# Routed expert outputs summed into one row per token by an accumulating indirect DMA

## The reference, cut to what matters

```
def hier_moe(h, ...):                 # h: 2048 x 1024
    grp    = argmax(h @ w_rg + b_rg)              # one of 4 groups
    gate_g = softmax(...)[grp]
    top_v, top_i = top_k(logits of the group's 8 experts, 2)
    w_top  = softmax(top_v) * gate_g[:, None]     # two weights per token
    expert = grp * 8 + top_i                      # 2 of 32 experts
    ...                                           # pairs sorted by expert, padded to blocks of 128
    def expert_block(tok, e):                     # 128 tokens of one expert
        xb  = h_pad[tok]
        hid = silu(xb @ w_gate[e]) * (xb @ w_up[e])      # 1024 -> 512
        return hid @ w_down[e]                           # 512 -> 1024
    out = zeros.at[slot_tok].add(yb * slot_w[:, None])   # each token gets two weighted rows
x = x + g2 * rmsnorm(out, norm_post_ffn)
```

## Time and profile before

| | us |
|---|---|
| median of 3 runs | 2709.36 |
| lowest and highest run | 2709.01, 2710.21 |
| the profiled execution: time | 2709.29 |
| the profiled execution: span, first to last instruction | 2707.6 |
| PE, DVE, ACT, POOL busy in the span | 2294.0, 1419.3, 1097.3, 652.7 |
| residual, from 1367 | about 305 |
| experts, its head without PE work, then its blocks | 22.2, then 905.6 |
| combine | 99.8 |

### The profile page before, as it was taken

How to read it: one execution, slowest core, us unless ns; L and a number is a source line. 1 busy time by engine, 2 the same in 40 slices (tenths; PEclk the granted TensorE clock), 3 DMA queues, 4 the chain that set the end, 5 groups by cost and what they waited for, 6 DMA issues and landing times. The chain is left out here.

```text
span 2707.6 us, 36235 instructions
## 1 busy us (share of the span) xinstructions
PE 2294.0 (85%) x11848; PEld 1888.1 (70%) x11849; DVE 1419.3 (52%) x1825; ACT 1097.3 (41%) x1597; POOL 652.7 (24%) x727
## 2 busy tenths in 40 slices
PE   5899997999994726799968993999999999999930
PEld 2688887999994316688856882777777777777730
DVE  2333332111112876687855775384766655538857
ACT  2433333222320321455532322475666555547821
POOL 0000000000001336588721323222122112112322
PEclk9899998999996869899988995999999999999975
DMA  7222224112125759655444332397788867649968
GB/s 257 87 93 93 93 93 133 47 67 74 48 80 181 292 180 354 225 185 182 145 147 175 133 125 96 113 367 257 242 291 289 286 205 264 226 158 325 367 236 319
DMA packets 297390, 509.48 MB, mean 188 GB/s; under 512 B 35760, under 2 KB 210256, under 8 KB 295120
## 3 DMA queue, kind: packets, MB, share of 16 engines
q1 hardware_dynamic: 263904, 403.20, 43.1%
q0 software_dynamic: 21904, 63.54, 6.6%
q10 hardware_dynamic: 11520, 41.95, 3.8%
HBM read 408.16 MB, written 110.43 MB: 192 GB/s over the span
## 5 line engine op out<-in xcount | busy, mean ns | idle before, releaser
L2171 DVE TENSOR_TENSOR e_w_low<-e_w_whole,e_w_high 128x2048 fp32r<-128x2048 f32 x192 | 432.0, 2292 | 82.7 <-ACT e_w_high L2127 82.3
L2127 ACT ACTIVATE e_w_high<-e_w_whole 128x2048 fp32r<-128x2048 f32 x192 | 356.4, 1909 | 17.6 <-PEq L1516 12.3
L2081 PE MATMUL e_pG<-e_w_high,e_xT 128*128 128x512 f32 x768 | 305.0, 397 | 1.2 <-ACT e_xT L2120 1.2
L2082 PE MATMUL e_pG<-e_w_low,e_xT 128*128 128x512 f32 x768 | 305.1, 397 | 0.0
L610 PE MATMUL proj_acc<-w_high,hT_high 128*128 128x512 f32 x672 | 266.1, 396 | 6.9 <-DVE hT_low L645 5.7
L610 PE MATMUL proj_acc<-w_low,hT_high 128*128 128x512 f32 x672 | 263.2, 392 | 0.0
L610 PE MATMUL proj_acc<-w_high,hT_low 128*128 128x512 f32 x672 | 263.1, 391 | 0.0
L2100 PE MATMUL e_pY<-e_w_high,e_hT 128*128 128x512 f32 x768 | 221.6, 400 | 0.0
L2085 PE MATMUL e_pG<-e_w_high,e_xT 128*128 128x512 f32 x768 | 194.9, 395 | 0.0
L306 POOL TENSOR_TENSOR stat<-stat,eps 128x1 f32<-128x1 f32 x36 | 10.8, 299 | 728.2 <-ACT xn L514 728.2
L2081 PEld LDWEIGHTS e_pG<-e_w_high,e_xT 128*128 128x128 f32 x768 | 145.2, 189 | 36.8 <-issue 1.6
(11 more groups left out here) (290 smaller groups left out, 4414.1 us busy)
## 6 DMA issues: line engine op xcount, KB each, us to landing
e_w_whole<-in_moe_w_gate_dram SPq DMA_DIRECT2D x64, 1024.0 KB, 7.7
e_w_whole<-in_moe_w_up_dram SPq DMA_DIRECT2D x64, 1024.0 KB, 10.8
e_w_whole<-in_moe_w_down_dram SPq DMA_DIRECT2D x64, 1024.0 KB, 9.4
xt<-in_x_dram SPq DMA_DIRECT2D x32, 512.0 KB, 5.4
wm_rest<-in_w_mod_dram POOLq DMA_DIRECT2D x8, 2048.0 KB, 12.2
c_yy<-rows_done SPq DMA_DIRECT2D x32, 512.0 KB, 7.4
by_token<-tok SPq DMA_DIRECT2D x16, 768.0 KB, 5.6
m_tok<-by_token SPq DMA_DIRECT2D x16, 768.0 KB, 4.2
```

The source lines that it names most:

```text
L2081: nc.tensor.matmul(pG[:, half], xT[:, 0, k], wh[:, half, w], start=(k == 0), stop=False)
L2082: nc.tensor.matmul(pG[:, half], xT[:, 0, k], wl[:, half, w], start=False, stop=False)
L2127: nc.scalar.activation(wh[:, third, part], raw[:, third, part], ACT.Copy).then_inc(whs.sem, 1)
L2171: nc.vector.tensor_tensor(wl[:, third, part], raw[:, third, part], wh[:, third, part].bitcast(F32), ALU.subtract).then_inc(wls.sem, 1)
```

## The change

The DRAM list `ids` gets a third integer per slot, the bits of the router's weight (IDS = 3). Empty slots are now (SKIP, 2048 + a row of its own for each of 128 partitions, 0). `ys` has 2048 + 128 rows, one for a token and 128 spare ones; it is filled with zeros at the start of `residual`. Each block scales its hidden rows by the weight of their slot and adds its 128 result rows, those of empty slots too (to the spare rows), to `ys` by an indirect DMA with `compute_op=ALU.add`. The gather skips empty slots. `combine` loads one row of sums per token, has four slots of each buffer, and no weighted sum.

```diff
@@ residual: constants, POOL
+            sp.dma_start(spare[:], io["rel"][:, 2, :]).then_inc(spare_in.sem(0), 16)
             sp.dma_start(iota[:], io["iota8"]).then_inc(o_in.sem(0), 16)
...
-            nc.gpsimd.memset(none[:, :, 0], 0).then_inc(zeroed.sem, 1)
-            nc.gpsimd.memset(none[:, :, 1], SKIP).then_inc(zeroed.sem, 1)
+            nc.gpsimd.memset(none[:, :, 0], SKIP).then_inc(zeroed.sem, 1)
+            nc.gpsimd.memset(none[:, :, 2], 0).then_inc(zeroed.sem, 1)
+            nc.gpsimd.memset(zero[:], 0.0).then_inc(zeroed.sem, 1)
...
             pool.wait_ge(zeroed.sem, zeroed.at(0))
-            pool.dma_start(dram["ids"].rearrange("(p n) o -> p (n o)", p=P), none[:].rearrange("p n o -> p (n o)")).then_inc(ids_init.sem(0), 16)
+            pool.wait_ge(spare_in.sem(0), spare_in.at(0))
+            nc.gpsimd.tensor_scalar(none[:, :, 1], spare[:], float(SEQ - 1), None, ALU.add).then_inc(spared.sem, 1)
+            pool.wait_ge(spared.sem, spared.at(0))
+            for part in dram["ids"].rearrange("(q p n) o -> q p (n o)", q=4, p=P):
+                pool.dma_start(part, none[:].rearrange("p n o -> p (n o)")).then_inc(ids_init.sem(0), 16)
+            halves = dram["ys"].rearrange("(p a) (h d) -> p (a h) d", p=P, h=2)
+            pool.dma_start(halves, zero[:].unsqueeze(1).to_broadcast([P, halves.shape[1], D // 2])).then_inc(ys_init.sem(0), 16)
             pool.wait_ge(o_in.sem(0), o_in.at(0))
@@ residual: DVE, place
-                link(V.reciprocal(g["wtop"][:, 0, r:r + 1], dn[:]))
-                link(V.tensor_tensor(g["wtop"][:, 1, r:r + 1], g["wtop"][:, 0, r:r + 1], ex[:, s], ALU.mult))
+                w0, w1 = (token[:, r, k, 2:3].bitcast(F32) for k in range(2))
+                link(V.reciprocal(w0, dn[:]))
+                link(V.tensor_tensor(w1, w0, ex[:, s], ALU.mult))
@@ experts: POOL
-                pool.indirect_dma_start(xb[:], None, dram["h2"], bass.IndirectOffsetOnAxis(ap=ids[:, 0:1], axis=0)).then_inc(x_in.sem(0), 16)
-            nc.gpsimd.memset(ids[:], SKIP).then_inc(none.sem, 1)
-            nc.gpsimd.memset(held[:], SKIP).then_inc(none.sem, 1)
+                pool.indirect_dma_start(xb[:], None, dram["h2"], bass.IndirectOffsetOnAxis(ap=ids[:, 0:1], axis=0), bounds_check=SEQ - 1, oob_is_err=False).then_inc(x_in.sem(0), 16)
+            nc.gpsimd.memset(xb[:], 0.0).then_inc(none.sem, 1)
             nc.gpsimd.memset(y[:], 0.0).then_inc(none.sem, 1)
+            pool.dma_start(held[:, 0:1], io["tokens"][:, 0:1], allow_slow_non_contiguous=True).then_inc(none_in.sem(0), 16)
+            pool.wait_ge(none_in.sem(0), none_in.at(0))
+            for at in (ids[:, 1:2], held[:, 1:2]):
+                nc.gpsimd.tensor_scalar(at, held[:, 0:1], SEQ, None, ALU.add).then_inc(none.sem, 1)
             pool.wait_ge(none.sem, none.at(0))
+            nc.gpsimd.tensor_copy(held[:, 0:1], held[:, 1:2]).then_inc(spared.sem, 1)
+            pool.wait_ge(spared.sem, spared.at(0))
...
-                pool.indirect_dma_start(dram["ys"], bass.IndirectOffsetOnAxis(ap=held[:, 1:2], axis=0), y[:], None, bounds_check=2 * SEQ - 1, oob_is_err=False).then_inc(y_out.sem(0), 16)
+                pool.indirect_dma_start(dram["ys"], bass.IndirectOffsetOnAxis(ap=held[:, 1:2], axis=0), y[:], None, compute_op=ALU.add).then_inc(y_out.sem(0), 16)
...
                 pool.wait_ge(xTt.sem, xTt.at(b - 1))
+                pool.wait_ge(weighed.sem, weighed.at(b - 1))
@@ experts: DVE
-                    nc.vector.tensor_tensor(hid[:, half * 256:(half + 1) * 256], sg[:, half], pG[:, half, 1], ALU.mult).then_inc(hids.sem, 1)
+                    if half == 0:
+                        dve.wait_ge(weighed.sem, weighed.at(b))
+                    nc.vector.scalar_tensor_tensor(out=hid[:, half * 256:(half + 1) * 256], in0=sg[:, half], scalar=weight[:, 0:1], in1=pG[:, half, 1], op0=ALU.mult, op1=ALU.mult).then_inc(hids.sem, 1)
...
+                weigh(b + 1)
                 if following is not None:
                     low(following, 1)
...
+            def weigh(b):
+                dve.wait_ge(hids.sem, hids.at(b - 1))
+                dve.wait_ge(x_in.sem(0), x_in.at(b))
+                nc.vector.tensor_copy(weight[:], ids[:, 2:3].bitcast(F32)).then_inc(weighed.sem, 1)
@@ combine
-    B = 3
+    B = 4
...
-                for k in range(2):
-                    sp.dma_start(yy[:, t % B, k], dram["ys"][k * SEQ + t * P:k * SEQ + (t + 1) * P, :]).then_inc(y_in.sem(t % B), 16)
+            for t in range(NL):
                 if t >= B:
                     sp.wait_ge(outs.sem, outs.at(t - B))
+                sp.dma_start(yy[:, t % B], dram["ys"][t * P:(t + 1) * P, :]).then_inc(y_in.sem(t % B), 16)
                 sp.dma_start(x1[:, t % B], dram["x1"][t]).then_inc(x_in.sem(t % B), 16)
...
-                nc.vector.tensor_scalar(v[:, s], yy[:, s, 0], g["wtop"][:, 0, t:t + 1], None, ALU.mult).then_inc(summed.sem, 1)
-                dve.wait_ge(summed.sem, summed.at(t, 1))
-                nc.vector.scalar_tensor_tensor(out=v[:, s], in0=yy[:, s, 1], scalar=g["wtop"][:, 1, t:t + 1], in1=v[:, s], op0=ALU.mult, op1=ALU.add).then_inc(summed.sem, 1)
```

More of the change, by code:

```diff
@@ L50 @@
 SKIP = 1 << 20
+IDS = 3
 EPS = 1e-6
@@ L1666, in _ @@
                 nc.gpsimd.tensor_scalar(token[:, :, k, 0], row[:], 0, None, ALU.add).then_inc(ruled.sem, 1)
-                nc.gpsimd.tensor_scalar(token[:, :, k, 1], row[:], k * SEQ, None, ALU.add).then_inc(ruled.sem, 1)
+                nc.gpsimd.tensor_scalar(token[:, :, k, 1], row[:], 0, None, ALU.add).then_inc(ruled.sem, 1)
             def body(t, use, s):
@@ L1918, in experts @@
         wl = kit.sb("e_w_low", [P, 3, THIRD], F32R, stack=st)
-        ids = kit.sb("e_ids", [P, 2], I32, stack=st)
+        ids = kit.sb("e_ids", [P, IDS], I32, stack=st)
+        weight = kit.sb("e_row_weight", [P, 1], stack=st)
         held = kit.sb("e_rows_held", [P, 2], I32, stack=st)
@@ L1936, in experts @@
         taken = kit.counter("e_rows_taken")
-        none = kit.counter("e_rows_none", 3)
+        none = kit.counter("e_rows_none", 4)
+        spared = kit.counter("e_rows_spared")
+        none_in = kit.landing("e_spare_rows_in")
+        weighed = kit.counter("e_row_weight_on", 1, credit=1)
         whs = kit.counter("e_w_high_ready", 6)
@@ L2158, in _ @@
         def _(dve):
-            for x_ in (xTl, hids, hTl, yd, wls):
+            for x_ in (xTl, hids, hTl, yd, wls, weighed):
                 dve.sem_inc(x_.sem, x_.credit)
@@ L2272, in finish @@
                 nc.vector.tensor_tensor(v[:, s], v[:, s], x1[:, s], ALU.add).then_inc(outs.sem, 1)
-            for t in range(NL + 1):
-                if t < NL:
-                    add(t)
-                if t >= 1:
-                    finish(t - 1)
 def program(nc, io):
```

57 lines of the change are left out of this document (29 added, 28 removed).

## The result

The changed kernel takes 2752.57 us (median of 4 runs, 2747.61 to 2754.70); the kernel before, beside it on the same chip, 2709.78. The ratio is 1.0153, 95% interval 1.0136 to 1.0171: slower by 43 us, where 2722 was forecast and 2750 was the upper end of the range. The profiled execution took 2754.51 us, its span 2752.9.

A forecast was written before the change was run, and what follows sets the result against it. PE was taken to bound the expert blocks, with DMA bounding combine and nearly full in heavy runs. Terms -23 + 2.5 + 5 + 1.5 + 2 + 0 + 25 = +13 on 2709.3 gave 2722 us; 8-in-10 range 2692 to 2750.

The forecast's parts named there:

- the wait for the weight: POOL's pairs' load in expert blocks also waits for DVE's copy; only a run's first block pays, within slack: 0.
- The accumulating scatter: Expert blocks: the add's read of the destination takes DMA time, 1.42 us a block, felt in heavy runs: +25 us.
- the reserve: Runs of heavy blocks: about 3.2 us of extra DMA demand can be absorbed before a run slows.
- POOL's loop becomes the bound: Rival, expert blocks: the add's later landing lengthens POOL's loop to some 21.7 us; total +36, 2745 us; chance 0.18.
- Combine: Last stage: a tile moves 1.57 MB instead of 2.10, priced at 393 GB/s: -23 us, between -18 and -25.
- Head of experts: Before the first expert block: extra small load, instructions and first scatter, partly offset by a faster pairs' load: +5, +2 to +12.
- Tail: End of experts: the last scatter is exposed, writing 128 rows and reading as many: +2.5 us, 0.5 to 6.
- Start of residual: Zeros of 8.9 MB, spare-row instruction and four list DMAs, mostly fitting idle DMA time: +1.5 us, 0 to +10.
- DVE in the blocks: Product with `up` becomes a three-operand instruction, 0.06 us more in each of 31 heavy blocks: +2 us.

The follow-up runs named there:

- e_weigh_late: Changed kernel, pairs' load not waiting for the weight; POOL copies the weight aside behind the scatter's issue, gather still behind the landing; 2709.79 us, 0.9997.
- e_plain_weigh: Changed kernel with plain writes instead of adds and no wait for the weight ahead of the pairs' load (POOL's copy ahead of the scatter); 2703.70 us, 0.9981.
- e_plain: Changed kernel with all row scatters as plain writes of the same 128 rows instead of adds, same waits; 2718.32 us, 1.0013.
- e_plain_both: Changed kernel with plain writes instead of adds, the gather waiting neither for the weight nor for the scatter's landing; 2685.72 us, 0.9902.
- e_skip_weigh_late: e_weigh_late with the adding scatters also skipping the spare rows, some 85 rows instead of 128; 2697.95 us, 0.9954.
- c_three: e_both with three slots instead of four in combine; 2702.74 us, 0.9968.
- e_skip_only: Changed kernel with one edit, its adding scatters skip the spare rows by a bound on the row; 2731.10 us, 1.0074.
- e_ahead: Changed kernel, adds and wait for the weight kept, rows held in three columns so the gather doesn't wait for the scatter's landing; 2707.82 us, 0.9983.
- e_both: Changed kernel with adds, the pairs' load and gather waiting neither for the weight nor for the scatter's landing; 2704.82 us, 0.9970.
- e_skip: e_both with its adding scatters also skipping the spare rows by a bound on the row; 2701.36 us, 0.9961.
- e_weigh: Changed kernel with adds, pairs' load not waiting for the weight; POOL copies the weight aside between the gather's and the scatter's issue; 2757.13 us, 1.0162.

## Why the prediction was wrong, step by step

The direction came out right and the size did not. The step that failed is "the wait for the weight", put at **0**. The argument was that in a heavy run the pairs are asked for later than DVE's copy would allow, so that only a run's first block pays, "within the gather's slack of 2 to 3 us". The delay was 2.6 us at that place, near the 2.5 of the step, and POOL waited for the weight 26 times. What the step missed is that in a heavy run the loop had no slack for it: the scatter's landing, the moves of the held rows, the pairs and the gather are one chain as long as a block, and the delay that entered it came out three times as long at the place shown (2.6 to 7.9), as POOL's instructions behind it took longer and the add landed later. The step's worth is 42.8 us beside an add by the medians, 47.2 in the blocks (e_weigh_late against the changed kernel), and 14.6 or 27.7 beside a write (e_plain_weigh against e_plain). Some 5 of it are the 0.1 us more in each of the 48 blocks. It is not a sum of parts: any of three edits, no wait, the landing out of the loop, or no add, gives back 27 to 47 us, and all three together (e_plain_both) 59.9.

That the direction was right is luck. The forecast's "slower" came from the +25 of the add; with the add as it is and no wait for the weight (e_weigh_late) the ratio is 0.9997, no slower than before. The loss came from the step at 0, and two sizes that were too pessimistic, the add and `combine`, together some 20 us, hid part of it.

*The accumulating scatter*, +25. The read does take the engines' time, 1.7 us per scatter where the step had 1.42. The Trainium skill says of a reduce-scatter that its add needs two source reads where a copy needs one ("Collectives: The Full Stack", section "The bandwidth ceiling: the fold count and why AG ≠ RS ≠ AR"); the queue's 284 us against 199 agree with that. The size was too large: in the blocks 14.7 us over the kernel before in e_weigh_late, perhaps some 6 more by its median, and 11.9 against plain writes. The runs of heavy blocks lost less than the step had, that of 8 11.1 us and not 13.1, of 5 4.2 and not 7.0, of 3 0.4 and not 2.9, as if the reserve were larger than 3.2 us. And the mechanism is not shown: the last run's 20.75 us a block (2535.14 to 2576.64 in two) are near the step's 18.88 + 2.04 = 20.92, but with a third of the rows skipped the pace stays at 20.8 (e_skip_weigh_late), and the whole of POOL's loop is as long. In the changed kernel ACT waits for weights 11 us in all where it waits 31 in e_weigh_late: PE's stalls seem to have given the DMA engines time, which is argued, not shown.

*POOL's loop becomes the bound*, the rival at 0.18, came nearest in time (2745), and its sign, PE waiting for `e_x`, is what the changed kernel's waits show. Its cause was not the whole: it named the add's later landing alone, and with that landing still in the loop 42.8 us come back once the wait for the weight is gone. That landing, at a median of 9.7 us in e_weigh_late, costs PE 9.9 us in 9 waits when the weight is not waited for.

*Combine*, -23, measured -32.9 and outside the step's -18 to -25. Bytes were priced at the 393 GB/s of its middle; the whole stage before moved 33.6 MB in 99.8 us, 337 GB/s, and after 25.2 MB in 66.9, 377. The mean rate of the stage, which was in the same row, would have given -25 for the bytes. The rest goes with a share of the engines that rose from 0.89 to 0.94 and a rate in the middle that rose from 393 to 419 GB/s. The slots have no part in it (c_three). Whether DVE's shorter chain is the reason was not tried by itself.

*Head of experts*, +5 with 2 to 12: +7.9, from 23.0 to 30.9. The first scatter was 10.6 us longer than before, where the step had 3 to 5, and the pairs' load gave 3.2 back. With plain writes (e_plain) the head is 29.3, with no row moved (e_skip_only) 27.5. So the add itself is 1.6 of the 7.9, the write of the rows 1.8, and 4.5 are the small load, the instructions and the place behind the weights that they gave the scatter: even without rows it took 8.9 us (1680.42 to 1689.35 in e_skip_only). The step counted the load and the instructions, but not that place. *Tail*, +2.5: +3.9; with a plain write of the same 128 rows it is 7.6 us, with the add 11.3, so nearly all of it is the add's and 0.2 the rows'. *Start of residual*, +1.5: +1.8.

*DVE in the blocks*, +2: nothing. In every kernel without the wait for the weight, the product on DVE unchanged, light and heavy blocks take 18.36 and 18.9 us as before. The 0.1 us more per block goes with that wait (also in e_plain, e_ahead and e_skip_only); by what way I did not find.

What stays open: why skipping a third of the adds' rows gave nothing in the blocks once the landing was out of the loop (920.1 and 919.4), though it gave 15 us in the changed kernel and 4.4 in e_weigh_late (11.8 by the medians, some 3 of them in the head). The queue's time in the DMA engines fell by 52 us between e_both and e_skip, and the median landing from 10.4 to 9.0 us, as with plain writes (8.9), so neither of the two makes the 11.9 us of the add by itself. What e_both and e_skip share is ACT's wait for weights, 12.8 and 15.0 us, against 3.0 with plain writes; by what way an add of few rows delays the weights I did not find.

## What to carry to other kernels

Before a wait is put into an engine's program, add up the whole serial chain it joins, landings included, and compare it with the period that it must keep: if the two are equal, even 2 us are not "within the slack", and the delay can come out larger than it went in. An experiment that takes a delay out of such a chain must not put an instruction of its own in: e_weigh and e_weigh_late differ only in the place of one small copy and its wait, and by 47 us in time. Where an add replaces a write, count the destination's read as DMA time, and let nothing wait for its landing that need not. Before a stage's first DMAs are moved, see which large loads they will then stand behind.

## What the hardware showed that was not expected

An adding scatter of 128 rows costs 1.7 us more of the DMA engines' time than a plain one with the same packets and bytes, and the profile's bytes (73.96 MB in the queue in both, 399.86 MB read from HBM in both) don't show its read. Alone, at the end of the stage, it was 10.6 us from issue to the next stage's first load (2675.47 to 2686.03); the plain one of e_plain took 6.8 (2645.34 to 2652.11):

```profile
2675.47 1.58 POOL L2052 DMA_INDIRECT rows_summed<-e_y,e_rows_held  x1 [7.64 <-DVE e_y L2221]
2686.03 0.34 SPq L2268 DMA_DIRECT2D c_yy<-rows_summed  x1
```

```profile
2645.34 0.99 POOL L2052 DMA_INDIRECT rows_summed<-e_y,e_rows_held  x1 [11.24 <-DVE e_y L2221]
2652.11 0.34 SPq L2268 DMA_DIRECT2D c_yy<-rows_summed  x1
```

A copy of one column on POOL lasts 0.18 us, or about 2 when DVE is in one of its 2.3 us splits: 1786.09 in the changed kernel and 1776.78 in e_weigh_late, above. The copy ends with the split: at 1788.13 behind a pair that ends at 1788.08, and in e_weigh_late at 1776.61 (1776.29 and 0.32) behind one that ends at 1776.56. In the heavy runs the issue of an indirect DMA also stretches, the gather's from 1.05 us in a light block (at 1749.29) to 2.93 at 1770.90.
